# A hybrid decoder layer on one core: bias matrix by load, later keys from tokens in a row, first up-projection units interleaved, first down step moved forward

## What is computed

```
z  = rms_norm(h) @ w_in          # q, k, v of 3 groups x 4 heads x 128, and more columns
for g, (window, dilation) in enumerate(((128, 1), (512, 4), (2048, 16))):
    k = rms_norm(k[:, g]) ; q = rms_norm(q[:, g])      # over each head's 128
    scores = q k^T * 128**-0.5 + bias[g]               # keys t - j*dilation, j = 0..window//dilation
    o[g], lse[g] = softmax(scores) v
A = groups combined per head by their softmax denominators
M = cross-attention into 256 memory tokens ; C = gated depthwise convolution module
h = h + W_out(sig(g_A)*P_A(A) + sig(g_C)*P_C(C) + sig(g_M)*P_M(M))
a, gt = causal_conv3(rms_norm(h) @ w_up)               # 1024 -> 2 x 2816
h = h + (silu(gt) * a) @ w_down
```

## Time and profile before

| | us |
|---|---|
| device time, median of 3 runs (1883.08 to 1886.47) | 1884.33 |
| the profiled execution's own time | 1883.33 |
| its span, first to last instruction | 1881.4 |
| PE busy | 1859.3 (99%) |
| DVE busy | 1194.5 (63%) |
| ACT busy | 764.9 (41%) |

### The profile page before, as it was taken

How to read it: one execution, slowest core, us unless ns; L and a number is a source line. 1 busy time by engine, 2 the same in 40 slices (tenths; PEclk the granted TensorE clock), 3 DMA queues, 4 the chain that set the end, 5 groups by cost and what they waited for, 6 DMA issues and landing times.

```text
span 1881.4 us, 23722 instructions
## 1 busy us (share of the span) xinstructions
PE 1859.3 (99%) x8790; PEld 1597.3 (85%) x8790; DVE 1194.5 (63%) x1636; ACT 764.9 (41%) x1420; POOL 86.7 (5%) x150
## 2 busy tenths in 40 slices
PE   7999999999999999999999999999999999999999
PEld 6788999999998888888888888878888888888887
DVE  5535753674373788897415625478777787867675
ACT  7423532352253146213613422365454544544443
POOL 1101110111010010000100000000000000000000
PEclk9999999999999999999999999999999999999999
DMA  7422432133222101102103415112323232267543
GB/s 256 146 90 68 141 118 90 41 129 112 90 91 98 50 33 46 45 23 68 45 23 98 151 45 179 56 56 68 101 67 100 67 100 67 76 212 264 164 140 101
DMA packets 133972, 184.15 MB, mean 98 GB/s; under 512 B 15929, under 2 KB 63033, under 8 KB 133881
## 3 DMA queue, kind: packets, MB, share of 16 engines
q1 hardware_dynamic: 125575, 172.24, 28.1%
q10 hardware_dynamic: 8306, 10.68, 1.6%
HBM read 142.92 MB, written 39.96 MB: 97 GB/s over the span
## 4 chain that ended last, share of the span: by engine, by line
PE 90%; DVE 6%; ACT 2%; issue 1%; ACTq 0%; DMA 0%; DVEq 0%
PE psum L240 29%; PE psum L241 28%; PE psum L242 28%; DVE wlo L198 2%; PE psum L871 1%; PE psum L531 1%; PE psum L1095 1%; DVE softstat L1264 1%; ACT sc L1174 1%; DVE sc L1262 0%; PE psum L872 0%; DVE pt_lo L1285 0%; DVE act_lo L397 0%; DVE acc L990 0%; DVE acc_odd L990 0%
## 5 line engine op out<-in xcount | busy, mean ns | idle before, releaser
L240 PE MATMUL psum<-whi,act_lo 128*128 128x512 f32 x768 | 315.7, 411 | 2.0 <-DVE q_lo L545 0.9
L242 PE MATMUL psum<-whi,act_hi 128*128 128x512 f32 x768 | 304.5, 397 | 0.0
L241 PE MATMUL psum<-wlo,act_hi 128*128 128x512 f32 x768 | 304.4, 396 | 0.0
L240 PEld LDWEIGHTS psum<-whi,act_lo 128*128 128x128 f32 x768 | 194.8, 254 | 17.6 <-DVE wlo L198 2.2
L242 PEld LDWEIGHTS psum<-whi,act_hi 128*128 128x128 f32 x768 | 195.0, 254 | 15.4
L241 PEld LDWEIGHTS psum<-wlo,act_hi 128*128 128x128 f32 x768 | 195.9, 255 | 12.9
L240 PE MATMUL psum<-act_hi,wlo 128*128 128x512 f32 x512 | 202.2, 395 | 0.0
L242 PE MATMUL psum<-act_hi,whi 128*128 128x512 f32 x512 | 199.7, 390 | 0.0
L241 PE MATMUL psum<-act_lo,whi 128*128 128x512 f32 x512 | 199.4, 389 | 0.0
L193 ACT CAST whi<-stage 128x512 fp32r<-128x512 f32 x200 | 119.8, 621 | 173.8 <-PE psum L242 165.9
L198 DVE TENSOR_TENSOR wlo<-stage,whi 128x512 fp32r<-128x512 f32 x200 | 129.9, 686 | 93.0 <-ACT whi L193 92.2
(11 more groups left out here) (255 smaller groups left out, 3507.3 us busy)
## 6 DMA issues: line engine op xcount, KB each, us to landing
stage<-in_w_in SPq DMA_DIRECT2D x144, 256.0 KB, 3.9
u_raw<-in_w_up SPq DMA_DIRECT2D x44, 512.0 KB, 5.0
stage<-in_w_down SPq DMA_DIRECT2D x44, 256.0 KB, 3.6
w_sums<-stage SPq DMA_DIRECT2D x44, 256.0 KB, 2.5
gated_scratch<-g_buf SPq DMA_DIRECT2D x22, 512.0 KB, 2.6
gated<-gated_scratch SPq DMA_DIRECT2D x44, 256.0 KB, 4.0
d_raw<-w_sums SPq DMA_DIRECT2D x44, 256.0 KB, 2.7
d_raw<-in_w_down SPq DMA_DIRECT2D x33, 256.0 KB, 3.5
```

Of the source, the lines that this page charges most:

```text
L240: nc.tensor.matmul(dst, lhs[1], rhs[0], start=first, stop=False, skip_group_check=True)
L241: nc.tensor.matmul(dst, lhs[0], rhs[1], start=False, stop=False, skip_group_check=True)
L242: return nc.tensor.matmul(dst, lhs[0], rhs[0], start=False, stop=last, skip_group_check=True)
```

## The change

Five edits:

1. The bias matrix. `bias_lines` is copied in DRAM 128 times per line (`bias_rows`, one transfer of 2.36 MB), and each group's `bias` is loaded from it by rows that start one number earlier each. The mirror's load, its product on the PE and DVE's copy are gone.
2. Keys of groups 1 and 2 are computed from 128 tokens in a row, and sorted on writing: each tile writes 32 (or 16) columns at each of 4 (or 8) places of every head. ACT does it in one instruction, DVE in four. All eight tiles now wait until the group before has taken its last scores. The tile at t = 3 goes to PSUM bank 4, and six weight splits stand before the last key tile's square and sum instead of four.
3. Memory stage: the line of group 1 goes to bank 7 and waits for no copy; DVE scales the first keys two splits earlier.
4. Up projection: product 6 of unit 1 stands between products 5 and 3 of unit 0. The code of units 0 and 1 on ACT and DVE is written out in a new order, and the last two of the activation sums swap.
5. Product 2's first step of the down projection stands between products 5 and 3 of the last unit, and DVE makes its low parts ahead of the gating product of the unit before.

```diff
@@ gemm_bank
+            if i in (3 * NT + 3, 6 * NT + 3):
+                return 4
@@
+        def group_cols(a, g, t):
+            r = (1, 4, 8)[g]
+            return a.rearrange("q h (r p) -> q h p r", r=r)[:, :, t * P // r:(t + 1) * P // r, :]
@@ norm_dve_lo
-            nc.vector.scalar_tensor_tensor(lo, norm_heads(n), vecs[:, wcol:wcol + 1], hi.bitcast(F32), ALU.mult,
-                                           ALU.subtract).then_inc(hn_lo, 1)
+            src = norm_heads(n, r)
+            for h in range(NH) if r > 1 else [slice(None)]:
+                step = nc.vector.scalar_tensor_tensor(lo[:, h], src[:, h], vecs[:, wcol:wcol + 1], hi[:, h].bitcast(F32),
+                                                      ALU.mult, ALU.subtract)
+            step.then_inc(hn_lo, 1)
@@ bias_line
-            else:
-                pe.wait_ge(lines_copied, g)
-            nc.tensor.matmul(psum[0:NH, 3, 0:LINE], ...
+            elif g == 2:
+                pe.wait_ge(lines_copied, 1)
+            nc.tensor.matmul(psum[0:NH, line_bank(g), 0:LINE], ...      # 7 for g == 1, else 3
@@ memory_stage vector
-                splits_dve(dve, 1, 0, 4)
+                splits_dve(dve, 1, 0, 2)
                 norm_dve_scale(dve, 0, 0, mem_qn)
-                splits_dve(dve, 1, 4, 6)
+                splits_dve(dve, 1, 2, 6)
@@ Tile
-                self.lhs = act_tile(slice(t * P, (t + 1) * P)) if kind == "X" else group_tile(g, t)
+                self.lhs = act_tile(slice(t * P, (t + 1) * P)) if kind in "KX" else group_tile(g, t)
@@
+        def first_part(tl):
+            return {"V": RING - 1, "K": RING - 2 if tl.g else RING // 2, "Q": RING // 2, "X": RING // 2}[tl.kind]
@@ tiles_pe
-                    if tl.kind == "V" and tl.t == 0:
-                        pe.wait_ge(bias_loaded, 16 * (tl.g + 1))
-                        ...
-                            mm = nc.tensor.matmul(psum[:, 3 + j, :], mirror_sb[:], ...
-                        mm.then_inc(bias_flipped, 1)
@@ tiles_act
-                    free = (s_done, NT * tl.g if tl.t else NT * (tl.g - 1) + 2) if tl.g else None
+                    free = (s_done, NT * tl.g) if tl.g else None
@@ attention sync
+                        lines = bass.AP(bias_lines.tensor, 0, [[LINE, NG * NH], [0, P], [1, LINE]])
+                        sp.dma_start(bias_rows.rearrange("g h p i -> (g h) p i"), lines).then_inc(bias_copied, 16)
                     load_turn(turn_k + 2)
+                    if g == 0:
+                        sp.wait_ge(bias_copied, 16)
+                    else:
+                        sp.wait_ge(s_read, NT * g)
+                    shifted = bass.AP(bias_rows.tensor, g * NH * P * LINE + P - 1,
+                                      [[LINE - 1, P], [P * LINE, NH], [1, 2 * P]])
+                    sp.dma_start(bias[:], shifted).then_inc(bias_loaded, 16)
@@ up_stage tensor
                 up_pe_5(pe, 0, 0)
+                up_pe_6(pe, 1, 1)
                 ...
                 up_pe_3(pe, 0, 0)
                 ...
                 up_pe_4(pe, 0, 0)
-                for U in (1, 2):
-                    middle(pe, U, U % 2)
+                middle(pe, 1, 1, True)                                 # without its product 6
+                middle(pe, 2, 0)
                 ...
                 up_pe_5(pe, LAST, 1)
+                pe.wait_ge(c12_done, NU - 1)
+                pe.wait_ge(c21_done, NU - 1)
+                down_pe(pe, 0, 0)
                 up_pe_3(pe, LAST, 1)
```

More of the change, by code:

```diff
@@ L573, in build, with line_bank @@
         X_FIRST = 3
+        def line_bank(g):
+            return 7 if g == 1 else 3
         def bias_line(pe, g):
@@ L1030, in tiles_pe @@
                         bias_line(pe, 2)
-                    if tl.kind == "V" and tl.t == 0:
-                        pe.wait_ge(bias_loaded, 16 * (tl.g + 1))
-                        if tl.g >= 1:
-                            pe.wait_ge(s_read, NT * tl.g)
-                        for j in range(2):
-                            mm = nc.tensor.matmul(psum[:, 3 + j, :], mirror_sb[:],
-                                                  hankel[:, 2 * j:2 * j + 2, :].rearrange("p h c -> p (h c)"),
-                                                  start=True, stop=True)
-                        mm.then_inc(bias_flipped, 1)
                 else:
@@ L2392, in build, with down_pe @@
         FIRST_STEPS = 4
+        BANKS_E, BANKS_A = (0, 1, 2, 5), (3, 4, 6, 7)
+        PRODUCT = {2: (BANKS_E, True, None, 1), 1: (BANKS_A, True, None, 1), 7: (BANKS_E, True, 0, 4),
+                   6: (BANKS_A, False, 1, 3), 4: (BANKS_E, False, 2, 3), 5: (BANKS_A, False, 3, 4),
+                   3: (BANKS_A, False, 5, 2)}
+        def down_pe(pe, n, k):
+            bank_set, fresh, read, _ = PRODUCT[DOWN_ORDER[n]]
+            step = n * W_HALF + k
+            pos = step % SLOTS
+            pe.wait_ge(gs_lo_done, step + 1)
+            pe.wait_ge(w_lo[step % 2], LO0 + step // 2 + 1)
+            for t in range(4):
+                if k == 0 and read is not None:
+                    pe.wait_ge(out_ready, 4 * read + t + 1)
+                if k == 0 and n == 0 and t == 3:
+                    pe.wait_ge(c11_done, NU)
+                if k == 0 and n == 1 and t < 2:
+                    pe.wait_ge((c21_done, c12_done)[t], NU)
+                tok = slice(t * P, (t + 1) * P)
+                mm = three(pe, psum[:, bank_set[t], :], (a_hi[pos][:, tok], a_lo[pos][:, tok]),
+                           (d_hi[pos][:], d_lo[pos][:]), fresh and k == 0, k == W_HALF - 1)
+                if k == W_HALF - 1 and t < 3:
+                    mm.then_inc(down_done, 1)
+            mm.then_inc(w_freed, 1)
         def up_stage():
@@ L2405, in sync, with middle @@
                     up_store(sp, U, U % 2)
-            def middle(pe, U, par):
-                up_pe_6(pe, U, par)
+            def middle(pe, U, par, second=False):
+                if not second:
+                    up_pe_6(pe, U, par)
                 up_pe_7(pe, U, par)
@@ L2505, in pair_dve @@
                 np = 1 - par
[L2506 removed]
+                second = isinstance(U, int) and U == 1
                 last = isinstance(U, int) and U == LAST
+                if second:
+                    up_dve_lo(dve, U + 1, np, 1)
                 up_c11(dve, U, par)
[L2509 to L2510 removed]
+                if not last:
+                    for n in range(2 if second else 0, 3):
                         up_dve_sum(dve, U + 1, half_next, np, n)
[L2512 to L2514 removed]
+                up_dve_lo(dve, U, par, 3)
+                if not last:
                     up_dve_sum(dve, U + 1, half_next, np, 3)
[L2516 to L2521 removed]
+                up_dve_lo(dve, U, par, 4)
+                if not last and not second:
+                    up_dve_lo(dve, U + 1, np, 1)
+                up_taps(dve, 0, U - 1, np)
                 if last:
[L2523 to L2524 removed]
+                    down_lows(dve, 0)
+                up_product(dve, U - 1, np)
+                if last:
+                    down_lows(dve, 1)
                 if not last:
```

165 lines of the change are left out of this document (71 added, 94 removed).

## The result

The changed kernel takes 1873.34 us in the median of six runs (1872.8 to 1875.22), against 1884.55 us before in the same comparison: a ratio of 0.9943, 95% interval 0.9933 to 0.9954. Timed again later it took 1870.71 (1869.96 to 1873.58) against 1884.49, ratio 0.9925 (0.9912 to 0.9939). Predicted were 1869.0 us and 15.3 us of gain. The granted clock, as a mean over each run, tells the two comparisons apart: in the first it is 0.999 or 0.998 in all six runs, in the second 1.000 in the four runs of 1869.96 to 1870.91 and 0.999 in the slowest. The profiled execution took 1873.44 us, 9.9 less than that of before, so 5.4 us of the sum are missing in it.

The account below looks back on a forecast made before the run. The PE, busy 99% of the time, was taken as the bound. Gains 5.2 + 4.9 + 1.0 + 3.6 + 0.6 = 15.3 us took 1883.3 to 1868.0, on the median 1.0 higher, 1869.0 us; range 1863 to 1876.

Parts of the forecast that it names:

- B: Rival, key writes of groups 1 and 2: sorted writes pay for their steps, 3.2 us less gain, 1872.2 us; 17%.
- C: Rival, unit 1 of the up projection: the clock falls in the new wait, 1.4 us more, 1870.4 us; 12%.
- Bias matrix: Each group's mirror product, 1.72 us on the PE, goes; three of them, 5.2 us less.
- The estimate for the copy: Bias copy of 2.36 MB in DRAM takes 24 us, 32 by the skill's rule; cost to the sum taken as 0.
- Keys: Key tiles of groups 1 and 2 gain 6.4 us from tokens in a row, less 0.8 and 0.75: 4.9 us.
- the term for the writes: Second key step of groups 1 and 2: sorted writes run as dense ones, addition 0.9 late, waits of 0.25 and 0.5 us.
- the wait of 0.5 us forecast for group 2: PE's wait for `pt_lo` before its transposes in group 2's second key step, 0.5 us (0.25 in group 1).
- Memory stage: The copied line's wait goes with its restart, 0.9; earlier scaling gives 0.1, as DVE waits for the norm anyway: 1.0 us.
- Units 0 and 1: Up projection: three PE waits go, a gain of 3.6 us, with a new wait of some 1.7 before unit 1's product 4.
- A: Rival, up projection: DVE doesn't bound unit 1, 2.0 us more gain, 1867.0 us; 10%.
- Last unit: First down step moved into the last unit covers a wait of 0.84 us with restart: gain 0.6, between 0 and 0.84.
- the weights of the ninth down step (step 8): Down projection: these weights, ready at 1689.3 with the PE there at 1689.2, cost some 0.2 us of wait.

Follow-up runs that it names:

- experiment 7: Changed kernel with keys of groups 1 and 2 sorted on reading PSUM and SBUF written in runs; key stretches 61.65 and 58.59 us, 1.4 shorter.
- experiment 4: Changed kernel with down step 0's low parts behind unit 20's gating product; 214.32 us from product 4 on. Its table lists weight cut against step 4 wait by kernel.
- experiment 10: The kernel before the change with only the bias matrix edit (bias by load); 1877.93 us.

## Why the prediction was right or wrong

The range of 1863 to 1876 held the time, and the direction was right. Part of this is luck. Of the 5.4 us that are missing in the profile, 2.1 are in the memory stage and 2.3 in the tail, and no rival had either; the range was wide enough for other reasons (B and C). Rival B's 1872.2 lies nearest the first median, but what it described took 1.4 us and not 3.2. In the four runs that kept the full clock the kernel took 1870.0 to 1870.9, 1 to 2 us above the forecast. By its steps:

1. *Bias matrix*: right, 5.15 for 5.2, and the PE waits for no transfer in V of group 0. The estimate for the copy was more than twice too long, 24 us for some 11; nothing hung on it.
2. *Keys*: 4.0 for 4.9. The gain of the matmuls was right. Mis-sized was the term for the writes: for "it runs as a dense one" ACT's takes 1.72 times as long (1.174 against 0.683), each of DVE's four 0.447 us against 0.342 when sorted on reading. From the end of the last scores (228.2) to the bias addition (230.89) it is 2.7 us, not the 1.9 that I worked out. Another term hides 0.5 of this: with the writes at the price that I had assumed (experiment 7) the gain was 5.4, not 4.9, since the wait of 0.5 us forecast for group 2 did not come. Rival B, at 17%, had the mechanism and for ACT the size (+0.5); for DVE it took 1.1 where 0.36 was measured (1.48 against 1.12), and the whole is 1.4, not 3.2. The Trainium skill (SBUF — State Buffer, section Door 1: The DMA port swizzle) had said that an access that goes to another line of 16 bytes pays, and ACT's writes agree with it (1.17 us with the step against 0.68 without), DVE's too. I had set it against the absence of such a row, which was no evidence for the dense price.
3. *Memory stage*: right at equal landing (1.05 for 1.0). Missing was that DVE's wait for the norm hung on the landing of x, which scatters by 1.4 us, and that a longer wait of the PE there was followed by the half clock. I had called DVE's wait harmless without asking what it waited for.
4. *Units 0 and 1*: right, 3.56 for 3.6, with the new wait of 1.69 for 1.7 and the clock up. Rivals A and C did not come: in none of the ten profiles with this wait (1.65 to 1.69 us) did the clock fall.
5. *Last unit*: wrong, a loss of 0.2 to 3.3 us in seven profiles for a gain of 0.6. The step that failed is the one that followed DVE's last gating product to "the weights of the ninth down step (step 8)". These were in time: ACT cut them at 1676.29, and the PE came to step 8 near 1680. Behind that product stand the low parts of step 4. Moving a step of 2.72 us ahead of product 4 takes 2.72 us of cover from the chain that begins with the copy of product 3; before, the chain had 0.8 to spare and could move up by 0.95, which leaves 0.92 of wait, as measured. The two low parts moved ahead of the gating product (1.2 us) delay store and load of step 3; with a late landing this added up to 1.5 more, by the table of experiment 4. I had named this side of the move only as "now stand ahead of the product".

## What to carry to other kernels

When a piece of work is moved forward on the bound engine, the work that it passed is pushed back, and what hangs on that work loses as much cover before the steps behind the old place: go through each consumer there in order, not only the one whose load is known to be late. Sort on the side of PSUM, in reading, and write SBUF in runs: here ACT's write took 0.68 us so and 1.17 the other way. Where a short chain at the start needs nothing of a large load, put it ahead of the work on that load in the engine's order. The kernel with this and the other repairs spread over 0.6 us instead of 3.6.

## What the runs showed of the hardware

The same load of x in the same place landed between 21.5 and 22.9 us, and one weight load in the tail was cut 5.7 to 7.6 us after the product that starts its chain, with SP's issue at the same distance each time. Neither scatter shows in one profile.

The clock did not follow the length of the wait alone. In the memory stage, where the short product of the bias line (0.81 us on 33 partitions) stands ahead of the wait, it fell to the lower level in all three profiles with a wait of 1.26 us or more and in none up to 1.20. In unit 1 it stayed full after 1.65 to 1.69 us ten times out of ten. In the tail it fell after 2.03, 2.20 and 2.42 us and not after 2.39. Before product 3 of unit 0 it fell after 2.58 and again after 2.56 in experiment 10. Each time it cost 1.4 to 1.6 us beyond the wait. What decides between 2.39 and 2.03 us is open.
